# Start addresses of the split weights: high rows 16 bytes, low rows 40 bytes past a multiple of 256

## The reference, cut to what matters

```python
z = xn @ w_in[l] + b_in[l]                      # 1024 x 1536
h = h + y @ w_out[l]                            # 1024 x 1024
(jax.nn.silu(x @ w_gate) * (x @ w_up)) @ w_down # 1024 x 2816, twice, and 2816 x 1024
proj = x @ w_in                                 # attention: queries, keys, values
u = x @ w_in                                    # second feed-forward: 1024 x 5632
return (jax.nn.silu(g) * val) @ w_out           # 2816 x 1024
```

## Time and profile before

| what | value |
|---|---|
| runs | 1811.86, 1812.83, 1810.9 us |
| profiled execution | 1808.84 us, its span 1807.0 us |
| mean granted TensorE clock | 0.994 of 2.4 GHz |
| TensorE matmuls | busy 1762.7 us (98%), 8755 |
| TensorE weight loads | busy 1476.5 us (82%), 8755 |
| VectorE | busy 765.9 us (42%), 1382 |
| ScalarE | busy 796.0 us (44%), 1674 |
| POOL | busy 1032.3 us (57%), 926 |
| DMA | 171.94 MB, mean 95 GB/s, the engines busy for a third of the span |

### The profile page before, as it was taken

One profiled execution on the slowest core, in us unless ns is written; L12 is line 12 of the kernel. 1 busy time (PEld: TensorE's weight loads), 2 busy tenths in 40 slices (PEclk: granted clock), 3 DMA queues, 4 the chain that ended last, 5 costly groups with the idle time before them and its releaser, 6 DMA issues.

```text
span 1807.0 us, 26859 instructions
## 1 busy us (share of the span) xinstructions
PE 1762.7 (98%) x8755; PEld 1476.5 (82%) x8755; DVE 765.9 (42%) x1382; ACT 796.0 (44%) x1674; POOL 1032.3 (57%) x926
## 2 busy tenths in 40 slices
PE   8999999999999999999999999999999999999997
PEld 6879888888887888788888888877777888888887
DVE  7973000001235556553333322487875533333224
ACT  5644332322245555464444422555565644444231
POOL 6966555555562333466666665655554666666651
PEclk9999999999999999999999999999999999999999
DMA  4312333333334454223333233333332233332332
GB/s 153 94 47 82 105 93 93 93 88 109 94 89 115 126 134 120 85 75 100 103 94 93 82 110 88 82 93 78 86 82 71 72 110 97 93 101 82 105 91 98
DMA packets 327252, 171.94 MB, mean 95 GB/s; under 512 B 43458, under 2 KB 316948, under 8 KB 327188
## 3 DMA queue, kind: packets, MB, share of 16 engines
q1 hardware_dynamic: 327172, 171.12, 33.7%
q10 hardware_dynamic: 16, 0.00, 0.0%
HBM read 152.15 MB, written 2.10 MB: 85 GB/s over the span
## 4 chain that ended last, share of the span: by engine, by line
PE 86%; DVE 9%; ACT 2%; issue 1%; POOL 1%; DMA 0%; DVEq 0%; SPq 0%; ACTq 0%
PE bank L983 24%; PE bank L985 23%; PE bank L984 23%; DVE score L2266 3%; PE attended L983 2%; PE attended L984 2%; PE attended L985 2%; PE turned L1424 1%; PE attended L1440 1%; PE bank L1056 1%; PE bank L1068 1%; DVE xres L2165 1%; PE bank L1069 0%; PE score L1417 0%; PE score L1407 0%
## 5 line engine op out<-in xcount | busy, mean ns | idle before, releaser
L742 POOL TENSOR_TENSOR WL<-raw,WH 128x512 fp32r<-128x512 f32 (+3 forms) x656 | 777.6, 1207 | 539.8 <-ACT WH L1605 537.2
L983 PE MATMUL bank<-XL,WH 128*128 128x512 f32 x1432 | 568.5, 397 | 3.7 <-DVE work L2577 1.2
L985 PE MATMUL bank<-XH,WL 128*128 128x512 f32 x1432 | 557.9, 390 | 0.0
L984 PE MATMUL bank<-XH,WH 128*128 128x512 f32 x1432 | 557.3, 389 | 0.0
L1605 ACT ACTIVATE WH<-raw 128x512 fp32r<-128x512 f32 (+3 forms) x656 | 338.4, 566 | 293.2 <-PE bank L985 186.5
L985 PEld LDWEIGHTS bank<-XH,WL 128*128 128x128 f32 x1432 | 269.4, 188 | 56.9
L983 PEld LDWEIGHTS bank<-XL,WH 128*128 128x128 f32 x1432 | 269.7, 188 | 55.9 <-DVE work L2577 1.5
L984 PEld LDWEIGHTS bank<-XH,WH 128*128 128x128 f32 x1432 | 269.9, 188 | 50.3
L983 PE MATMUL bank<-HL,WH 128*128 128x512 f32 (+1 forms) x528 | 198.6, 376 | 0.0
L985 PE MATMUL bank<-HH,WL 128*128 128x512 f32 (+1 forms) x528 | 198.4, 376 | 0.0
L984 PE MATMUL bank<-HH,WH 128*128 128x512 f32 (+1 forms) x528 | 198.4, 376 | 0.0
(11 more groups left out here) (366 smaller groups left out, 2524.9 us busy)
## 6 DMA issues: line engine op xcount, KB each, us to landing
raw<-in_ffn_w_in SPq DMA_DIRECT2D x88, 512.0 KB, 3.7
raw<-in_w_gate SPq DMA_DIRECT2D x22, 512.0 KB, 3.6
raw<-in_w_up SPq DMA_DIRECT2D x22, 512.0 KB, 3.7
raw<-in_ffn_w_out SPq DMA_DIRECT2D x28, 384.0 KB, 3.2
raw<-in_ffn_w_out SPq DMA_DIRECT2D x28, 320.0 KB, 3.2
raw<-in_a_w_in SPq DMA_DIRECT2D x16, 512.0 KB, 3.9
raw<-in_kv_w SPq DMA_DIRECT2D x32, 256.0 KB, 3.0
raw<-in_w_in SPq DMA_DIRECT2D x12, 512.0 KB, 3.7
```

What stands on the lines that cost most here:

```text
L742: pool.tensor_tensor(wl, x, wh, ALU.subtract).then_inc(w_lo, 1)
L983: pe.matmul(out_, wh, xl, start=start, stop=False)
L984: pe.matmul(out_, wh, xh, start=False, stop=False)
L985: return pe.matmul(out_, wl, xh, start=False, stop=stop)
```

## The change

`WH` and `WL` are each allocated 8 elements (32 bytes) longer, flat, and a view that skips some elements at the front takes the place of the tile: 4 elements (16 bytes) for `WH`, 2 (8 bytes) for `WL`. Since `WL` lies 32 bytes further on behind the longer `WH`, its view begins 32 + 8 = 40 bytes past a multiple of 256. `small` loses 16 elements (64 bytes), the sum of both additions, so that all that is allocated behind it stays where it was. `par`, `ones`, `identr`, `masks`, `work` and `small` itself begin 64 bytes later than before. The instructions, their order, their queues and their semaphores are the same.

```diff
-        WH = sb("WH", [P, SLOTS, DT, P], F32R)
-        WL = sb("WL", [P, SLOTS, DT, P], F32R)
+        WH, WL = (sb(name, [P, SLOTS * DT * P + 8], F32R)[:, skip:skip + SLOTS * DT * P].rearrange("p (s k c) -> p s k c", s=SLOTS, k=DT)
+                  for name, skip in (("WH", 4), ("WL", 2)))
...
-        small = sb("small", [P, 108 + 20])
+        small = sb("small", [P, 108 + 4])
```

## The result

Twenty runs of the changed kernel have a median of 1820.04 us, between 1809.75 and 1838.86; the kernel before has 1811.69 beside them. Changed to before, the ratio is 1.0050, 95% interval 1.0032 to 1.0068: slower by a small amount that is clear of the noise. (One run of the kernel before took twice the time, 3559.96 us; it counts in the median, which is 1811.6 without it, and neither it nor the changed kernel's longest, 1838.86, counts in the ratio.) The forecast, 1803 us, had the wrong direction. A second thing is new: the other nineteen runs of the kernel before lie within 0.4% of each other (6 us), those of the changed kernel spread over 29 us.

A forecast was written before the change was run, and what follows sets the result against it. TensorE's number of matmuls times the distance between starts was taken as the bound. -4.0 ns per triple times 2450 is -9.8 us, times 0.91 -8.9 us: 1799.9 against the profiled 1808.84, 1803 on the median; range 1778 to 1832.

The forecast's parts named there:

- TensorE bounds, the others add nothing: Whole kernel: TensorE holds 86% of the chain of waits; POOL, ScalarE, VectorE and the packing transfers were to change the time by zero.
- The addresses enter by a few ns per matmul, through the distance between a load and the rows beside it: Matmuls with low or high weights: start distances change spacing, -2.5 ns beside a high load, +1.0 beside a low one.
- The first rival, nothing happens: All these matmuls: the fixed 13.1 ns is a step between two sets of weights, blind to addresses; 1811.9 us, chance 0.28.
- The size at 256 columns: Weight-load triples: the forecast -4.0 ns per triple, applied to all 2450 triples, 388 of them 256 wide.
- a class that was to be slow: Starts at 8 modulo 16: 120.9 ns in the depthwise convolution, taken as 1.0 ns slower per low load.
- The class means of the convolution: Depthwise convolution, 90 spacings sorted by row start modulo 16: 117.4 ns at 0, 120.8 at 4, 120.9 at 8, 118.6 at 12.
- I carry this over by the distance between the load and the rows it runs beside: Convolution means applied to all 2450 triples, high loads as class 0, low as class 8: -4.0 ns per triple, -8.9 us.
- unshaken for 924 matmuls: Long loop from 180.20 to 389.64 us: constant 226.7 ns between starts, cited for the rival that nothing happens.
- the slower rival: Low loads, 8 bytes past a multiple of 16, each cost another 13.1 ns: 1830 us with the high weights' gain, 1841 without; chance 0.24.

The follow-up runs named there:

- the move alone: Kernel before with both weight tiles left at multiples of 256; only the tiles from the parameters to the small one begin 64 bytes later: 1809.85 us, ratio 0.9991.
- the 32-byte run: Kernel before with every tile, weights, streamed rows and all others, beginning 32 bytes later and all distances kept: 1810.69 us, ratio 1.0002.
- groups shifted as a whole by 8 or 16: Isolated matmul triples behind the last transfer of the kernel before, other engines idle, weights and rows all 8 or 16 bytes past multiples of 256: 690 to 700 ns.
- (8, 8): Isolated triples behind the kernel before, high and low weights both 8 bytes past a multiple of 256, rows aligned: 692 ns at 512 columns, 346.7 at 256.
- the aligned pair: High and low weights at multiples of 256, as in the kernel before; in isolated triples 680 ns at 512 columns in all eight entries, 360 at 256.
- (16, 40): The change's starts, high weights 16 and low 40 bytes past a multiple of 256; isolated triples 693.3 ns, or 700 entered from 256 columns; 353.3 at 256 columns.

## Why the prediction was wrong, step by step

**TensorE bounds, the others add nothing.** Right. POOL, ScalarE and VectorE have the durations of the earlier trace rows, the packing transfers land in 2.3 us as in the earlier trace rows, and the move alone is 0.9991.

**The addresses enter by a few ns per matmul, through the distance between a load and the rows beside it.** Right in part: the 32-byte run keeps the time with all distances kept, and the other distances that ran cost 0.4 to 1.8%. But groups shifted as a whole by 8 or 16 are slow at unchanged distances (690 to 700 ns per triple), so the distance is not the whole of it. The first rival, nothing happens, stood at 1811.9; shifting weights alone moved the distance between starts from 226.7 to as much as 233.3 ns, so the place of the weights does matter. Beside that rival the prediction had set a rule of the Trainium skill ("TensorE: Matmul & The Clock Gate", "Step-by-step: what each phase is for"): loading the next weights takes no read bandwidth from the running matmul. What the prediction drew from it, that the place of the weights can't matter, doesn't hold here; whether a load takes bandwidth from the running matmul no run shows.

**The size at 256 columns.** Right sign, too small: -4.0 ns per triple forecast, 3 x (117.7 - 119.9) = -6.6 measured, at most 2.6 us in all. Its parts are not borne out: the low load at 40 was to cost 1.0 ns, but low weights alone at 40 bring the same 117.8 as high weights alone at 16, and (8, 8), of a class that was to be slow, is among the quickest (346.7). The class means of the convolution, which the earlier trace rows frame, came from 256 columns too. The convolution, whose tiles stay, kept its spacings, as the prediction said: 34 of them from 92.29 to 96.36 us, 119.7 ns each on the mean.

**"I carry this over by the distance between the load and the rows it runs beside": this step failed.** It applied a mean of 256-wide matmuls to all 2450 triples, of which 2062 are 512 wide. There the same shift costs 0, 13.3 or 20 ns per triple (680, 693.3 or 700) where -4.0 stood. Its hidden premise was that a pair of addresses has one distance between starts. The rows of before could not show otherwise, since the aligned pair has only one: "unshaken for 924 matmuls" was a property of this pair and not of the machine. The scatter of the convolution's spacings was the hint that other pairs are less settled; I averaged it away by class. That the measured median, 1820.04, still lies inside the stated range of 1778 to 1832 is no merit of the mechanism: the range reached up there for the slower rival.

**The slower rival** had the side, and for the low weights alone nearly the size: 1841 forecast, 1835.72 measured. Its mechanism is refuted all the same. The spacing that holds the low load, from L984 to L985, was to grow alone; in the change all three become longer, and another one the most: 233.3 ns from L983, 230.9 from L984 and 229.2 from L985 (means over the second long loop; 226.7 before). With the low weights alone shifted it is the longest, 234.5, but the other two grow as well, to 231.6 and 229.4, so about half of the loss lies in them. High weights alone were to gain, but lost 0.4%, and both weights at 16, where every row still begins at a multiple of 16, lose more than the change. The prediction had weighed the 16-byte lines of the Trainium skill ("SBUF — State Buffer", "Specifications (TRN2)") for this; a row of 512 bytes from such a start touches as many of these lines as an aligned one, so they don't explain what that run lost, 1.7%.

**What stays open:** why the aligned pair has one pattern and other pairs several, and what in an entry picks one. The runs show that the same addresses give different patterns by entry and that a pattern holds for a thousand matmuls; no row shows the state behind it. Nor do they say whether reading the weights and reading the rows get in each other's way or something else is timed by both.

## What to carry to other kernels

Where triples of 512 columns like these bound the kernel, keep stationary and streamed tiles at distances of a multiple of 256 bytes, and their starts at multiples of 32; in this kernel some bytes of filler cost nothing (ratios 0.9991 and 1.0002), and the other distances that ran cost up to 1.8%. Don't carry a cost per address from one width to another: measure it at the width that dominates, behind the entries that the kernel has. Where the runs of one program suddenly spread, compare the same stretch over several profiles before looking for a cause in the program.

## What the runs showed of the chip that I had not expected

TensorE's matmuls with a weight load each fall into steady patterns that depend on start addresses: 680, 687, 693 to 696 or 700 ns per triple of 512 columns at a granted clock of 1.00. The changed program took different ones in its two traced executions, and kept each until the loop was left. At 256 columns shifted starts are mostly quicker than aligned ones: 346.7 ns per triple at (8, 8), 353.3 at (16, 40), against 360.
